# Layers written out, another order of opening and waits, and one tiled section for linear attention in a two-layer decoder trunk

## The reference, cut to what matters

```python
for l in range(DEPTH):                       # 2
    h = rms_norm(x, mix_norm[l])
    z = h @ w_in[l]
    c_q, c_kv, k_r, hq, hf, hi, hg, guv, gates = split_sizes(z, IN_SIZES)
    y_a = mla(c_q, c_kv, k_r, ...) @ w_branch_a[l]
    y_b = hgrn2(hq, hf, hi, hg, lower_bounds[l], hg_head_norm[l]) @ w_branch_b[l]
    y_c = gmlp(guv, ...) @ w_branch_c[l]
    g_a, g_b, g_c = jnp.split(jax.nn.sigmoid(gates), 3, axis=-1)
    x = x + (g_a * y_a + g_b * y_b + g_c * y_c) @ w_mix_out[l]
    h = rms_norm(x, xa_norm[l]); m = rms_norm(mem, mem_norm[l])
    x = x + cross_attn(h, m, xa_w_q[l], xa_w_kv[l], xa_w_o[l])
    h = rms_norm(x, ffn_norm[l])
    gt, up = jnp.split(h @ ffn_w_in[l], 2, axis=-1)
    x = x + (jax.nn.silu(gt) * up) @ ffn_w_out[l]
return rms_norm(x, final_norm)
```

```python
o_inter = einsum('bhck,bhkv->bhcv', qc * exp(b), state)       # b: cumulated log decay
attn = einsum('bhtk,bhtsk,bhsk->bhts', qc, decay, kc)
o = o_inter + einsum('bhts,bhsv->bhtv', attn, vc)
```

## Time and profile before

| | us |
|---|---|
| median of 3 runs | 2067.67 (2067.53 to 2067.87) |
| the profiled execution | 2067.64 |
| its span | 2065.8 |
| TensorE busy (matmuls) | 2054.1 |
| TensorE's weight loads | 1698.4 |
| VectorE busy | 1205.1 |
| ScalarE busy | 897.6 |

### The profile page before, as it was taken

One profiled execution on the slowest core, in us unless ns is written; L12 is line 12 of the kernel. 1 busy time (PEld: TensorE's weight loads), 2 busy tenths in 40 slices (PEclk: granted clock), 3 DMA queues, 4 the chain that ended last, 5 costly groups with the idle time before them and its releaser, 6 DMA issues.

```text
span 2065.8 us, 34676 instructions
## 1 busy us (share of the span) xinstructions
PE 2054.1 (99%) x12535; PEld 1698.4 (82%) x12535; DVE 1205.1 (58%) x1862; ACT 897.6 (43%) x1410; POOL 0.4 (0%) x5
## 2 busy tenths in 40 slices
PE   9999999999999999999999999999999999999998
PEld 8888887788888888888878888777888888888887
DVE  6768776665655544443276787766656555444332
ACT  7656544444444332322275665444544433232223
POOL 0000000000000000000000000000000000000000
PEclk9999999999999999999999999999999999999999
DMA  6323232244333333333243323222334323333331
GB/s 185 82 74 97 68 82 72 58 122 113 105 111 92 99 95 102 92 95 95 77 129 88 80 76 82 68 78 78 109 111 123 102 82 102 92 102 93 94 99 63
DMA packets 360840, 194.67 MB, mean 94 GB/s; under 512 B 29676, under 2 KB 350808, under 8 KB 360664
## 3 DMA queue, kind: packets, MB, share of 16 engines
q1 hardware_dynamic: 356280, 186.99, 32.7%
q10 hardware_dynamic: 4384, 5.38, 0.9%
HBM read 190.24 MB, written 2.10 MB: 93 GB/s over the span
## 4 chain that ended last, share of the span: by engine, by line
PE 97%; DVE 1%; issue 1%; DMA 0%; ACT 0%; DVEq 0%; SPq 0%; ACTq 0%
PE PS L653 27%; PE PS L654 27%; PE PS L655 27%; PE PS L687 4%; PE PS L949 1%; PE PS L899 1%; PE PS L828 1%; PE PS L741 1%; PE PS L740 1%; PE PS L739 1%; PE PS L904 1%; PE PS L928 1%; PE PS L840 0%; PE PS L709 0%; PE PS L707 0%
## 5 line engine op out<-in xcount | busy, mean ns | idle before, releaser
L1081 ACT ACTIVATE wH<-raw 128x1024 fp32r<-128x1024 f32 (+3 forms) x382 | 377.2, 988 | 832.2 <-PE PS L655 765.1
L653 PE MATMUL PS<-hH,wH 128*128 128x512 f32 x1568 | 614.2, 392 | 0.1
L655 PE MATMUL PS<-hH,wL 128*128 128x512 f32 x1568 | 610.4, 389 | 0.0
L654 PE MATMUL PS<-hL,wH 128*128 128x512 f32 x1568 | 610.3, 389 | 0.0
L1495 DVE TENSOR_TENSOR wL<-raw,wH 128x1024 fp32r<-128x1024 f32 (+3 forms) x382 | 432.0, 1132 | 194.2 <-ACT wH L1081 193.7
L653 PEld LDWEIGHTS PS<-hH,wH 128*128 128x128 f32 x1568 | 294.4, 188 | 61.7 <-issue 1.1
L655 PEld LDWEIGHTS PS<-hH,wL 128*128 128x128 f32 x1568 | 294.3, 188 | 61.5
L654 PEld LDWEIGHTS PS<-hL,wH 128*128 128x128 f32 x1568 | 294.5, 188 | 60.3 <-issue 0.5
L1456 DVE TENSOR_TENSOR gate<-PS,rh 128x512 f32<-128x512 f32 x92 | 63.6, 691 | 162.6 <-PE PS L655 162.2
L653 PE MATMUL PS<-fH,wH 128*128 128x512 f32 x352 | 136.9, 389 | 0.0
L654 PE MATMUL PS<-fL,wH 128*128 128x512 f32 x352 | 136.9, 389 | 0.0
(11 more groups left out here) (355 smaller groups left out, 2960.1 us busy)
## 6 DMA issues: line engine op xcount, KB each, us to landing
raw<-in_w_in SPq DMA_DIRECT2D x106, 512.0 KB, 3.9
raw<-in_ffn_w_in SPq DMA_DIRECT2D x88, 512.0 KB, 3.8
raw<-in_xa_w_kv SPq DMA_DIRECT2D x32, 512.0 KB, 3.8
raw<-in_ffn_w_out SPq DMA_DIRECT2D x32, 512.0 KB, 3.8
raw<-in_w_mix_out SPq DMA_DIRECT2D x16, 512.0 KB, 4.0
raw<-in_xa_w_q SPq DMA_DIRECT2D x16, 512.0 KB, 4.0
raw<-in_xa_w_o SPq DMA_DIRECT2D x16, 512.0 KB, 3.9
raw<-in_ffn_w_out SPq DMA_DIRECT2D x16, 384.0 KB, 3.4
```

What stands on the lines that cost most here:

```text
L653: nc.tensor.matmul(o, w0, xh(k0 + k), start=(first and k == 0), stop=False)
L654: nc.tensor.matmul(o, w0, xl(k0 + k), start=False, stop=False)
L655: ins = nc.tensor.matmul(o, w1, xh(k0 + k), start=False, stop=(last and k == kts - 1))
L1081: nc.scalar.activation(weights_of(n, wH, NS), weights_of(n, raw, NR), ACT.Copy).then_inc(*did("scalar", "hi", n))
```

## The change

- The layer loop of each engine is replaced by its two turns, one after the other. Waits are on constants. The weights of layer 1's first four units are split behind the last units of layer 0 (`next_splits` in place of `freed`). Lower bounds, angles, sines and the positions' DMA are there for layer 0 alone.
- Opening: SP's queue carries x's quarter 0, the vectors, the weights of unit 0, quarter 1, the weights of unit 1, quarters 2 and 3, and behind unit 3's weights the tables and mixer tables that ScalarE's queue carried. Unit 0 of layer 0 begins with the two blocks of x that are there, and the transposes of the other six stand between its passes. Two of the four stretches of `busy` remain.
- `lb` is cut in three steps: 0 where it was, 1 behind `spread`, 2 behind `angle` 0, each with its activation of ScalarE.
- Linear attention: the transposes of a head are one step (`hg_suft`, four of them, one bank); then `hg_inter` of the head before (the products with the states), both halves of `hg_attn`, and the rest of `hg_out` follow each other with no unit between. `hg_q` and `hg_rs` stand behind. VectorE's wait for `hg_out` moves from before the mask to before the sum.
- `qn` 1 goes ahead of `v`; in `mla_s` the two blocks of heads (0, 2) precede those of (1, 3); in `xv` ScalarE evicts before it splits.

The diff, cut to its core (counting of marks, the same for each engine, is left out):

```diff
-    p = [("sqs_last",), u("gv", 0), u("gv", 1), ("lb",), u("gv", 2), u("gv", 3), ("norm", "mix"), u("hf", 0), ("f_0", 0), ("spread",), ("angle", 0), ("gm_mean",), ("gm_ws",)]
+    p = [("sqs_last",), u("gv", 0), u("gv", 1), ("lb", 0), u("gv", 2), u("gv", 3), ("norm", "mix"), u("hf", 0), ("f_0", 0), ("spread",), ("lb", 1), ("angle", 0), ("lb", 2), ("gm_mean",), ("gm_ws",)]
...
-        p += [u("gate_c", 2 * h)] + ([("hg_out", h - 1), ("hg_q", h), u("y_c", 2 * h), ("hg_rs", h - 1), nxt[0]] if h else [u("y_c", 2 * h), nxt[0]])
-        p += [("hg_attn", h, 0)] + ([("f_0", n)] if more else []) + [u("gate_c", 2 * h + 1), ("hg_attn", h, 1)]
-        p += ([("f_1", n)] if more else []) + [nxt[1]] + ([("hg_norm", h - 1)] if h else []) + [("hg_state", h)] + ([("f_2", n)] if more else [])
+        p += [u("gate_c", 2 * h), u("y_c", 2 * h), nxt[0], ("hg_suft", h)] + ([("hg_inter", h - 1)] if h else [])
+        p += [("hg_attn", h, 0), ("hg_attn", h, 1)] + ([("hg_out", h - 1), ("hg_q", h), ("hg_rs", h - 1)] if h else [])
+        p += ([("f_0", n)] if more else []) + [u("gate_c", 2 * h + 1)] + ([("f_1", n)] if more else []) + [nxt[1]] + ([("hg_norm", h - 1)] if h else []) + [("hg_state", h)] + ([("f_2", n)] if more else [])
...
-    p += [... u("kn"), u("v"), u("qn", 1), u("gate_b", 1)]
+    p += [... u("kn"), u("qn", 1), u("v"), u("gate_b", 1)]
...
+        def next_splits(l, n):
+            places = [PLACE[n] + NS] + ([PLACE[n] + 1 + NS] if PLACE[n] + 1 == LEFT_OUT else [])
+            after_it = [(l, q) if q <= NU else (l + 1, q - NU - 1) for q in places if q != LEFT_OUT]
+            return [(ll, user(q)) for ll, q in after_it if ll < L]
...
-            with sp.Fori(0, L) as l:
+            for l in each_layer("sync"):
...
+                    if l == 0 and n == 0:
+                        sp.dma_start(*quarter(1)).then_inc(sem("x_in1"), 16)
+                    if l == 0 and n == 1:
+                        sp.dma_start(*quarter(2)).then_inc(sem("x_in2"), 16)
+                        sp.dma_start(*quarter(3)).then_inc(sem("x_in3"), 16)
...
+                    if first:
+                        for k in range(kts):
+                            pe.wait_ge(sem("mix_h_ready"), k + 1)
+                            for i in range(TT):
+                                for x_ in (hH, hL):
+                                    nc.tensor.matmul(tm_banks[i], x_[:, k, i * P:(i + 1) * P], wH[:, s, k * m:(k + 1) * m], ...)
+                        for kt in (2, 3):
+                            x_transposed(kt, X_BANK[kt])
+                        pe.wait_ge(*low_done(l, n))
+                        for i in range(TT):
+                            for k in range(kts):
+                                ins = nc.tensor.matmul(tm_banks[i], hH[:, k, i * P:(i + 1) * P], wL[:, s, k * m:(k + 1) * m], start=False, stop=False)
+                        ins.then_inc(*did("tensor", *me))
+                        for kt in range(4, KT):
+                            if kt >= 6:
+                                pe.wait_ge(*x_copied(kt - 4))
+                            x_transposed(kt, X_BANK[kt])
+                        return
...
-                        for c, i in enumerate(blocks):
-                            n = (i + 1) * P
-                            for hh in (0, 2, 1, 3):
+                        for e in range(2):
+                            for c, i in enumerate(blocks):
+                                n = (i + 1) * P
+                                for hh in (e, 2 + e):
...
-                        for q in freed(n):
-                            split(l, q)
+                        if name != "xv":
+                            for ll, q in next_splits(l, n):
+                                split(ll, q)
...
-                        if h:
-                            dve.wait_ge(*after(l, "hg_out", h - 1))
-                        elif half == 0:
+                        if h == half == 0:
                             dve.wait_ge(sem("mask_in"), l * 16 + 16)
                         dve.wait_ge(*after(l, "hg_attn", h, half))
...
+                        if h:
+                            dve.wait_ge(*after(l, "hg_out", h - 1))
                         dve.wait_ge(*own(l, "vector"))
                         V.tensor_reduce(attn[:, half], mprod[:].rearrange("p i n t -> p i t n"), AX.X, ALU.add)...
```

More of the change, by code:

```diff
@@ L255, in own, with found @@
-        def own(l, engine):
[L257 to L269, removed]
+        def found(l, step):
+            for k in ((l, step), (None, step)) if l is not None else ((None, step), (L - 1, step)):
+                if k in mark:
+                    return mark[k]
+            return "tensor", 1
@@ L276, in starts, with each_layer @@
         def starts(engine):
-            phase[0] = "before"
+            at_layer[0] = None
             count[engine] = 0
[L280 to L283, removed]
+        def each_layer(engine):
+            for l in range(L):
+                at_layer[0] = l
+                counted["begun"][(l, engine)] = count[engine]
+                yield l
         def ends(engine):
-            counted["total"][engine] = count[engine]
-            phase[0] = "after"
-            count[engine] = 0
+            at_layer[0] = None
@@ L570, in _, with reader_done @@
             starts("tensor")
-            readers, fresh = [None] * 8, [False] * 8
-            turn = [0]
+            readers = [None] * 8
+            for kt in range(KT):
+                readers[X_BANK[kt]] = (None, ("x_copied", kt))
+            turn = [2]
+            def reader_done(l, step):
+                return x_copied(step[1]) if step[0] == "x_copied" else after(l, *step)
             def take(l, step, reader, keep=False, held=None):
@@ L578, in take @@
                 turn[0] += not keep
-                if fresh[b]:
-                    pe.wait_ge(*before(l, *last_reader.get(b, ("x0", 0))))
-                elif readers[b] and held is not None:
+                if readers[b] and held is not None:
                     held.append(readers[b])
                 elif readers[b]:
[L585 to L588, removed]
+                    pe.wait_ge(*reader_done(*readers[b]))
+                readers[b] = (l, reader)
+                counted["bank"][(at_layer[0], step)] = b
                 return PS[:, b, :]
@@ L612, in _, with x_transposed @@
             pe.wait_ge(sem("ident_in"), 16)
-            for kt in range(KT):
-                if kt == 2:
-                    busy(8)
-                b = take(None, ("x_t", kt), ("x0", kt))
+            def x_transposed(kt, b):
                 if kt % 2 == 0:
@@ new lines, in _ @@
+            nc.scalar.preload_act_table_set("silu_and_others")
+            x_in(0)
+            high_in(0)
+            split(0, 0)
+            high_in(1)
+            for l in each_layer("scalar"):
+                if l == 0:
+                    act.wait_ge(*after(None, "cur", "start"))
+                    split(0, 1)
+                    for kt in range(2, KT, 2):
+                        x_in(kt)
+                        act.wait_ge(*x_copied(kt))
+                        high(l, "mix_last", kt, col("mix_norm", kt))
+                        act.wait_ge(*x_copied(kt + 1))
+                        high(l, "mix_last", kt + 1, col("mix_norm", kt + 1))
+                        if kt < 6:
+                            split(0, kt // 2 + 1)
+                else:
+                    act.wait_ge(*after(l - 1, "ev", "fo", 3))
+                    for k in (2, 3):
+                        high(l, "mix_last", k, col("mix_norm", k))
+                    act.wait_ge(*earlier(l, "vector"))
+                    for k in range(4, KT):
+                        high(l, "mix_last", k, col("mix_norm", k))
+                if l:
+                    mixer_tables(act, l)
```

331 lines of the change are left out of this document (148 added, 183 removed).

## The result

The changed kernel is slower. Its median is 2076.3 us (2074.4 to 2081.9 in 6 runs) beside 2067.9 us (2067.5 to 2068.1, 6 runs) for the kernel before on the same chip: ratio 1.0045, 95% interval 1.0036 to 1.0055. The forecast was 2057.6 us, 18.7 us away, and outside the range. The profiled execution took 2075.7 us with a span of 2073.6 us, 7.8 us longer than before.

What follows compares the result with a forecast made beforehand. The prediction took TensorE, with 97% of the chain, to bound the kernel. Its terms, -1.5 + 2.1 - 2.1 - 4.2 - 1.1 - 1.0 - 2.2 = -10.0 us, gave 2057.6 us, range 2054.5 to 2061.5.

Steps and rivals of the forecast that it cites:

- Part 1: Opening: with the DMA bytes reordered, the second unit of `gv` starts at 17.2 to 17.3 us, gain 1.5 us.
- Part 2: Lower bounds in three pieces: the gating mean comes later, so layer 0's first product of `hi` waits, loss 2.1 us.
- Part 3: Layer boundary: layer 1's first weights are split at the end of layer 0, gain 2.1 us.
- Part 4: Tiled sections of linear attention: merging saves changes of tile form and restarts, no operand is late, gain 4.2 us.
- rival (d): Merged sections: TensorE waits for instruction packets, 3.8 us in each of eight, 2088 us; chance 0.05, shared with other new waits.
- Part 5: Three small orders: `qn` 1 ahead of `v` gains 1.1 us, `xv` 1.0, `mla_s` with heads in pairs 2.2.

Runs made afterwards that it cites:

- e5: The changed kernel with the lower bounds back together after the second unit and the merged section cut in two, a unit between: 2057.8 us.
- e4: The changed kernel with the outputs and level halves apart again and the lower bounds back together after the second unit: 2059.9 us.
- e8: e5 with one unit moved behind the preceding head's norm transposes and the state products, so these follow the second level half directly: 2077.8 us.
- e3: The changed kernel with the three pieces of the lower bounds together again after the second unit: 2074.8 us.
- e7: e4 with 80 products added behind the first level half in every head, at different widths and so different speeds: 2134.5 us.
- e2: The kernel before, its layer loop and all its orders kept, with only the merged section put in: 2083.9 us.
- e1: The changed kernel with the preceding head's outputs and the two level halves apart again, a unit between each two: 2063.8 us.

## Why the prediction was wrong

**Part 1, opening: right, undersized.** First product of `gv` at 8.25 us (forecast 8.7), second unit at 16.39 (forecast 17.2 to 17.3, before 18.77). The 2.4 us lie just above the range of 0.8 to 2.2: 0.45 because the first product starts earlier, 0.4 because the sequence up to the second unit takes 8.14 us and not 8.5.

**Part 2, the lower bounds: right in place and mechanism.** The wait was 2.7 us where 2.1 was forecast, and VectorE's `gm_b` is its releaser. What I did not price is the clock: five products after it at 0.427 us. In the experiments the whole part is worth 3.9 us.

**Part 3, boundary: right.** From the last product of `fo` to the 25th start after it, 1041.13 to 1046.80, it takes 5.67 us, where it took 7.66.

**Part 4, the sections: this is the step that failed.** They cost 11.6 us (8.8 and 2.8) where 4.2 were to be gained. The saving of forms is real (0.35 and 0.67 us in the sections that run through; 2.1 us for e5 over e4, where 3 was expected: 2057.8 us, not 2057), and no operand was late. But rival (d) came true. I had it, with its point of decision (1.25 us a section), and dismissed it with one sentence: within a half, 96 passes go at 0.0087 us each, without a gap. That row shows the pace at which TensorE empties what lies ready, not the pace at which it is filled. 96 passes fit into what lies ready; of the six sections with 258, five did not, and of the two with 196 one did not. A section's need (516 instructions with its transposes, two packets) against the time a packet takes to come was the right comparison, and the two numbers stood side by side in the prediction: 4.4 us for the section, 3.8 us for a transfer. The price, 3.8 us in each of eight, was too high: part of the fetch runs beside the section's own products, so 1.4 to 2.8 us (in starts) were left, in six of eight. The chance of 0.05 was the real error; there was no row for a block of more than 96 passes, so the cost should have been bounded from both sides like any unknown operation.

**Part 5.** `v` and `xv` as forecast (1.2 and 1.1 us). `mla_s` gave 1.3 where 2.2 was forecast: from the first product of the two-block section to the next step it took 2.06 us before and takes 1.63 after (starts in the traces), so 0.43 at most is gained and not 0.55, and the stretches behind them lose 0.03 to 0.09 each. The timeline's row for it, to be held against the 2.13 us of the earlier trace rows:

```profile
338.55 1.70 PE L929 MATMUL PS<-kn,qn 64*128 64x128 f32 x16
```

The test that the prediction set itself ("I am wrong if TensorE waits inside a merged section") is what the first view of the profile after showed.

## What to carry to other kernels

Small tiled products that run at under 0.01 us a pass may stand only so many in a row. What counts is whether a block reaches two packet borders, 256 instructions apart, before the second packet is there. Blocks of 132 to 164 passes (264 to 328 instructions with the weight loads) ran through here, but for three in e8 that TensorE entered or crossed waiting; at 180 and 196 it depended on the place; and of those from 228 on only the last merged section of layer 1 ran through, in the changed kernel and in e3 (all at the full pace; e7's slower blocks apart). Group them to save changes of form, but put a unit of large products between two groups; e5 does this and keeps half of the saving. When a row shows a burst at high speed, ask from what store it is fed and how fast that is refilled before you make the burst longer. And when an order is changed, count what is queued behind each wait on VectorE and ScalarE, as at the mean of the gating branch and in e8.

## What the runs showed of the hardware

- TensorE's instructions come in packets of 16 KB, one for 256 instructions: all 38 stops without a semaphore lie on borders that come every 256 records, and 2560 more instructions in e7 brought ten more packets. If a block uses them up at 0.0087 us a pass, TensorE stops and resumes 2.3 to 2.9 us after the next packet's transfer starts. It does so in a loop over layers (e2) as in straight code.
- A stop or wait of 0.9 to 3.8 us can be followed by 3 to 12 large products at 0.427 us, the lower level of the clock, or by none. The Trainium skill ("TensorE: Matmul & The Clock Gate", Part 1) says that the array is throttled by default and that the number of slow products at a kernel's start varies from run to run. The runs here show such a variation later in a kernel: the changed kernel's six runs go from 2074.4 us at a mean granted clock of 0.998 to 2081.9 us at 0.995, where e5's four stay at 0.999 to 1.000 and within 0.3 us. A wait of 2.5 us in e1 without any slow product behind it shows that the wait alone doesn't decide.
- Passes of 32 columns cost 0.0087 us over four column groups and 0.034 us on one; 64 and 128 columns on one group cost 0.057 and 0.110 us.
